# Delta rule over the prompt: tanh and product of v in one piece of 1,024 tokens, or in two of 512

## The reference, cut to what matters

```
y, new_conv = causal_conv(concat([q_a, k_a, v_a]), conv_buf, conv_w)   # 4 taps, per channel
q, k, v = split(silu(y))                    # silu(y) = y * sigmoid(y)
q = l2norm(q) * GDN_DK ** -0.5;  k = l2norm(k)
o, S = gated_delta_rule(q, k, v, g, beta, S0)   # chunks; a triangular solve per chunk
o = rmsnorm(o, gdn_norm) * silu(z)
```

## Time and profile before

| | us |
|---|---|
| device time, median of 3 runs | 2988.15 |
| lowest and highest of the 3 | 2988.11 and 2989.14 |
| the profiled execution's own time | 2993.38 |
| its span, first to last instruction | 2991.6 |
| delta rule over the prompt, the seven full heads and the last | about 185 to 927 of the span |

### The profile page before, as it was taken

The page is one execution under the profiler, slowest core; times in us unless marked ns, Lnnn a source line. Parts: engine busy times, 40 slices in busy tenths (PEclk is TensorE's granted clock), DMA queues, the critical chain, the costliest instruction groups (busy, mean ns, idle before and its releaser), DMA issues. The chain is left out here.

```text
span 2991.6 us, 36429 instructions
## 1 busy us (share of the span) xinstructions
PE 2407.9 (80%) x12967; PEld 1973.2 (66%) x12968; DVE 1576.7 (53%) x2073; ACT 1108.7 (37%) x1574; POOL 420.3 (14%) x442
## 2 busy tenths in 40 slices
PE   4779988898876666799987999967928999999940
PEld 2478887798865443544447989966727888888710
DVE  2355556555552221134455465525437888888805
ACT  3233423332331100033333423313207777777602
POOL 1020212111222120012221000000022111111003
PEclk7899999999988667599998999988958999999965
DMA  7411112211213023111106544452248999999625
GB/s 289 171 39 45 44 31 60 55 33 32 59 32 111 29 70 116 43 43 42 42 1 229 152 122 136 137 179 86 80 178 305 403 406 402 405 402 402 242 105 190
DMA packets 315751, 444.63 MB, mean 149 GB/s; under 512 B 56659, under 2 KB 254819, under 8 KB 295892
## 3 DMA queue, kind: packets, MB, share of 16 engines
q1 hardware_dynamic: 291516, 379.32, 36.1%
q0 software_dynamic: 11168, 39.12, 3.6%
q10 hardware_dynamic: 13000, 25.30, 2.2%
HBM read 388.59 MB, written 57.14 MB: 149 GB/s over the span
## 5 line engine op out<-in xcount | busy, mean ns | idle before, releaser
L2541 DVE TENSOR_TENSOR ex_w_r<-ex_w,ex_wh 128x2048 fp32r<-128x2048 f32 x192 | 433.0, 2283 | 59.9 <-ACT ex_wh L2483 59.8
L2483 ACT ACTIVATE ex_wh<-ex_w 128x2048 fp32r<-128x2048 f32 x192 | 367.6, 1916 | 130.7 <-PEq L2190 43.1
L1868 PE MATMUL mg_psum<-mg_xl,mg_wh 128*128 128x352 f32 x768 | 252.1, 328 | 0.0
L1928 DVE TENSOR_TENSOR mg_w_r<-mg_w,mg_wh 128x1024 fp32r<-128x1024 f32 x96 | 129.6, 1355 | 127.6 <-ACT mg_wh L1881 127.4
L904 PE MATMUL gd_ps<-gd_hh,gd_wh 128*128 128x352 f32 x368 | 128.6, 349 | 62.2 <-ACT preS L624 62.2
L1881 ACT ACTIVATE mg_wh<-mg_w 128x1024 fp32r<-128x1024 f32 x96 | 101.4, 1057 | 184.4 <-DVE mg_out L1955 118.5
L1868 PEld LDWEIGHTS mg_psum<-mg_xl,mg_wh 128*128 128x128 f32 x768 | 148.4, 193 | 0.0
L1868 PE MATMUL mg_psum<-hT_r,mg_wh 128*128 128x352 f32 x384 | 127.6, 332 | 18.4 <-DVE mg_w_r L1928 18.4
L1564 PE MATMUL wp_proj_psum<-hT,wp_wq 128*128 128x512 f32 x256 | 116.2, 608 | 14.0 <-DMA wp_wk<-in_w_in_dram 8.8
L1868 PE MATMUL mg_psum<-hT_r,mg_w_r 128*128 128x352 f32 x384 | 125.7, 327 | 0.0
L904 PE MATMUL gd_ps<-hT_r,gd_wh 128*128 128x352 f32 x368 | 124.5, 338 | 0.0
(11 more groups left out here) (625 smaller groups left out, 5941.3 us busy)
## 6 DMA issues: line engine op xcount, KB each, us to landing
ex_w<-in_w_gate_dram SPq DMA_DIRECT2D x64, 1024.0 KB, 8.0
ex_w<-in_w_up_dram SPq DMA_DIRECT2D x64, 1024.0 KB, 7.4
ex_w<-in_w_down_dram SPq DMA_DIRECT2D x64, 1024.0 KB, 8.7
ada_w<-in_w_ada_dram SPq DMA_DIRECT2D x24, 1024.0 KB, 15.4
mg_w<-in_w_in_dram SPq DMA_DIRECT2D x48, 512.0 KB, 3.7
gd_w<-in_w_in_dram SPq DMA_DIRECT2D x32, 512.0 KB, 4.5
expert_out_scratch<-ex_y ACTq DMA_DIRECT2D x32, 512.0 KB, 7.6
mg_w<-in_w_br_gdn_dram SPq DMA_DIRECT2D x24, 512.0 KB, 4.1
```

What stands on the lines that cost most here:

```text
L1868: last = nc.tensor.matmul(pm[b][q][:, 0:R], a, x, start=(m == 0 and v == 0), stop=(m == KD - 1 and v == 2))
L1928: nc.vector.tensor_tensor(wl_r[q][:], wl[q][:], wh[q][:].bitcast(F32), ALU.subtract).then_inc(w_low, 1)
L2483: nc.scalar.activation(wh[at][:], wl[b][u][:], ACT.Copy).then_inc(w_high, 1)
L2541: nc.vector.tensor_tensor(wl_r[b][u][:], wl[b][u][:], wh[at][:].bitcast(F32), ALU.subtract).then_inc(w_low, 1)
```

## The change

The tanh of v becomes two instructions on ACT, each for 512 tokens, and each raises `v_tanh`. The product on DVE becomes two as well: each waits for its own half of the tanh and raises `v_silu`. On PE the wait for `v_silu` moves from ahead of the turn into it: the first four transposes wait for the first half, the last four for the second. The counts are adapted: `v_silu` rises by two per head, so `tanh_z` waits for twice the number. Nothing else is touched.

```diff
--- before.py
+++ after.py
@@ -648,7 +648,7 @@
 
                 def tanh_z(j):
                     act.wait_ge(z_evac, j * 3 + 3)
-                    act.wait_ge(v_silu, j)
+                    act.wait_ge(v_silu, j * 2)
                     nc.scalar.activation(th[2][:], zraw[:], ACT.Tanh, scale=0.5).then_inc(z_tanh, 1)
 
                 def body(i, nxt):
@@ -681,7 +681,9 @@
                         nc.scalar.activation(kt[g][:], X[g][0][:], ACT.Copy).then_inc(kts, 1)
                     act.wait_ge(v_conv, i * 4 + 4)
                     act.wait_ge(z_silu, i + 1)
-                    nc.scalar.activation(th[2][:], y[2][:], ACT.Tanh, scale=0.5).then_inc(v_tanh, 1)
+                    for g in range(2):
+                        at = slice(g * C4, (g + 1) * C4)
+                        nc.scalar.activation(th[2][:, at], y[2][:, at], ACT.Tanh, scale=0.5).then_inc(v_tanh, 1)
                     if nxt:
                         evac(0, 1, i + 1)
                         evac(0, 2, i + 1)
@@ -823,8 +825,10 @@
                         low(1, i + 1)
                     solve(i)
                     conv(2, i, 2, CONV)
-                    dve.wait_ge(v_tanh, i + 1)
-                    nc.vector.scalar_tensor_tensor(y[2][:], th[2][:], 1.0, y[2][:], ALU.add, ALU.mult).then_inc(v_silu, 1)
+                    for g in range(2):
+                        at = slice(g * C4, (g + 1) * C4)
+                        dve.wait_ge(v_tanh, i * 2 + g + 1)
+                        nc.vector.scalar_tensor_tensor(y[2][:, at], th[2][:, at], 1.0, y[2][:, at], ALU.add, ALU.mult).then_inc(v_silu, 1)
                     if nxt:
                         conv(0, i + 1, 0, 2)
                     for l in (4, 5):
@@ -998,9 +1002,9 @@
                             if l > 4:
                                 turn_tiles(X[g][1], Y[g]).then_inc(yturned, 1)
                         if l == 4:
-                            pe.wait_ge(v_silu, i + 1)
                             pe.wait_ge(capped, i * 8 + 8)
                             for g in range(2):
+                                pe.wait_ge(v_silu, i * 2 + g + 1)
                                 turn(pp[g], y[2], g).then_inc(vturned, 1)
                         elif nxt:
                             project(1, l - 4, 0, i + 1)
```

## The result

| | before | after |
|---|---|---|
| device time, median | 2989.41 us (8 runs, 2984.40 to 2992.69) | 2996.86 us (8 runs, 2992.43 to 3001.72) |
| the profiled execution's own time | 2993.38 us | 2997.69 us |
| ratio | | 1.0026, 95% interval 1.0014 to 1.0037 |
| both again, on another chip, median | 2992.41 us (35 runs) | 2995.02 us (12 runs) |
| ratio there | | 1.0003, 95% interval 0.9991 to 1.0014 |

The change made the kernel slower in the first comparison, by 7.5 us; the forecast was +0.7 us and its range ended at 2991.5. The second comparison shows no difference: its interval holds 1, and it holds the 1.0009 that the two medians give. The first lies outside the forecast's range. The median of the second does so too, but there the kernel before, with 2992.41 us, lies outside it as well.

What follows compares the result with a forecast made beforehand. PE bounds the kernel, waiting in each head for evacuations behind the tanh on ACT. The profiled 2993.38 us plus 0.7 for the tanh and 0 for product and wait gave 2994.1, or 2988.9 on the median; range 2986.3 to 2991.5.

Steps and rivals of the forecast that it cites:

- The critical path: Before the next head's first projection, PE waits for evacuations queued behind the tanh on ACT, idle 8.10 us.
- Tanh in halves: On ACT, the second piece delays the evacuations and so PE by 0.10 us in seven heads: 0.7 us, ends 0.2 and 1.4.
- Wait inside the turn: On PE, between the two groups of transposes, the wait is long passed: 0, at most 1.9 us in eight heads.
- Product in halves: On DVE, two products of about 1.15 us would end near 205.8 instead of 206.16: readiness gained, time 0.
- The cover of 5.67 us: Slack between the product's end on DVE and PE's turn of v; 4.10 us in the last head.
- The table load: Rival on ACT: a 1.28 us tanh table load comes before the evacuations, 9.0 us in all, 2997.9; chance 0.03.
- The clock's rival: In the heads, a small delay shifts PE's clock changes, 1.3 us per head tipped: 2987.6 to 2991.5; chance 0.10.
- Value 0: Time effect given to the product in halves on DVE and to POOL, which shares the stretch.
- a little for something unseen: Part, beside the table load, of the 0.04 chance of being slower by over 0.2%.
- Some scatter of the median: The 0.6 us taken off for the range's lower end, 2988.15 - 1.3 - 0.6 = 2986.3.
- the three runs agree within 1.03 us: Evidence given against the rival that a small delay tips heads between longer and shorter clock patterns.

Runs made afterwards that it cites:

- the eighths: The kernel before with the tanh of v in eight pieces of 128 tokens, the product whole and waiting for all: 3000.45 us, ratio 1.0029.
- The shift alone: The kernel before plus two one-element copies on ACT at the end of its delta rule stage, nothing of v split: 2993.14 us, ratio 1.0012.
- the split without it: The kernel after with two pairs of front-stage exponentials merged, so ACT's later program stands where it did before: 2990.08 us against 2988.94, ratio 0.9998.
- the pooled before: The unchanged kernel before, 110 runs pooled over the chips of the first five comparisons: mean 2990.4 us, standard deviation 5.1.

## Why the prediction was wrong

- **The critical path, right.** PE waits for the evacuations behind the tanh, not for the product. Moving them ahead gave 0.6%; the product in halves gave nothing; the turn never waited for the product.
- **Tanh in halves, right.** 0.10 us per head was forecast, 0.09 measured in every trace with two pieces and the old order, and the eighths carry it through to the heads' length.
- **Wait inside the turn, right.** 1.04 us for the eight transposes in seven heads, as before.
- **Product in halves, right in value, wrong in mechanism.** I expected two of 1.15 us, ending near 0.35 us earlier, because DVE and POOL both run slowly while they overlap. They took 2.67 together and ended 0.07 earlier; the shortest of the 16 takes 0.98 us, the longest 1.76. The rows show the two engines ending their instructions in turn instead, so that a second product waits for a second mask; where only the product is split, the pair ends 1.16 us later. The cover of 5.67 us was large enough that this changed nothing.
- **The table load, rightly given little.** It started 13.2 us ahead of the first tanh, as before (13.3).
- **The clock's rival, right in kind, in the wrong place.** In the heads its draws are worth some 3 us (676.4 to 679.9 us from first tanh to last, for kernels with and without the split). The large ones lie in stages that the prediction did not look at.
- **The step that failed: the sum has only terms of the stage that is edited.** "Value 0" was given part by part to instructions and waits, with no term for what the two more instructions do to the place of all that follows on ACT. That is 1.8 us in the overflow stage, where ACT had been 1.5 us short of being last. The shift alone measured +3.1 us (standard error 1.4), the split without it a ratio of 0.9998. None of the rivals named it; "a little for something unseen" was 0.01.
- **The second step that failed: the range.** "Some scatter of the median", 0.6 us, was taken from three runs within 1.03 us, and "against it that the three runs agree within 1.03 us" was used as evidence. The standard deviation of single runs is 5.1 us, over all chips. By that a median of 8 scatters by about 2 us, and the difference of two such by 3. Of the 7.5 us measured first, then, 0.6 is the tanh and 1.8 the empty rounds. The rest is part draw (the second comparison found 0.03%), part what stays open above: the mean over 20 runs is +4.2 us over the pooled before, standard error 1.1. With the 2.1 us of the merge stage the sum would be 4.5, but that the shift causes them is not shown.

## What to carry to other kernels

Before pricing an edit at nothing, look at loops of short rounds later in the program on the engines whose text grows, and at which engine ends last there by how little: here two more instructions were enough. Know the scatter of single executions before setting a range, from more than three runs, and compare a kernel with itself. And where an engine waits on the critical path behind an instruction that its reader does not need, move what the reader needs ahead of it (here 17 us) rather than cut the instruction into pieces.

## What the runs showed of the hardware

- An empty round of a skipping loop on ACT took 0.975 us at a shift of 0 instructions, 0.980 at 32, 1.11 at 2 and 8, 1.155 at 14, 1.167 at 16 (median over the rounds). At shifts of 0 and of 2 it is the same within 0.004 us in seven traces each. From the kernel before to the kernel after, 0.09 us of the difference comes after the backward branch, until the next round's first instruction starts (0.14 us against 0.23), and 0.04 after the branch that skips the body (0.17 against 0.21).
- A second ACT instruction of the same tanh, 512 elements instead of 1,024, costs 0.09 us of the queue, though each piece alone is shown with 0.62 us; eight pieces of 128 cost 0.64 more than one whole.
- DVE's product and POOL's masks end their instructions in turn. One whole product ended 3.40 us after the tanh's start, whether it started 1.09, 1.18 or 1.74 us after it; two halves took 2.67 us together behind a split tanh (0.98 and 1.76) and 3.47 behind a whole one, where the same product elsewhere takes 1.22 us whole.
- After an idle stretch of about 5 us, PE's matmuls at level 4 took twice their time (2.07 us for eight, where sixteen took 1.95), at a granted clock of 0.50, the lower of its two; what an earlier start gains is in part given back there.
